# A two-block network in split precision: the first weight unit behind each norm of block 2 computed without the root

## The reference

```python
def modulate(x, g, shift, scale):
    return rmsnorm(x, g) * (1 + scale) + shift
for i in range(2):
    x   = x   + 0.5 * gt1 * swiglu(modulate(x, g1, sh1, sc1), ffn1_wi[i], ffn1_wo[i])
    ctx = ctx + 0.5 * cg1 * swiglu(modulate(ctx, g1, ch1, cs1), ffn1_wi[i], ffn1_wo[i])
    hx, hc = modulate(x, g2, sh2, sc2), modulate(ctx, g2, ch2, cs2)
    # i = 0: pointwise GLU, depthwise convolution of width 31, LayerNorm, swish, pointwise
    # i = 1: windowed attention of 16 query and 4 key heads with a sink; latent queries only
    x   = x + gt2 * y_lat            # (i = 0: ctx + cg2 * y_ctx too)
    x   = x + 0.5 * gt3 * swiglu(modulate(x, g3, sh3, sc3), ffn2_wi[i], ffn2_wo[i])
    # (i = 0: ctx too)
return rmsnorm(x, final_g)
```

## Time and profile before

| What | Value |
|---|---|
| Median of 3 runs | 3044.67 us (3044.47 to 3045.72) |
| Profiled execution | 3043.92 us |
| Its span, first to last instruction | 3042.1 us |
| PE busy | 2997.0 us, 99% |
| DVE busy | 2116.9 us, 70% |
| ACT busy | 1303.8 us, 43% |
| Mean granted TensorE clock | 0.998 |

### The profile page before, as it was taken

One profiled execution on the slowest core, in us unless ns is written; L12 is line 12 of the kernel. 1 busy time (PEld: TensorE's weight loads), 2 busy tenths in 40 slices (PEclk: granted clock), 3 DMA queues, 4 the chain that ended last, 5 costly groups with the idle time before them and its releaser, 6 DMA issues.

```text
span 3042.1 us, 48628 instructions
## 1 busy us (share of the span) xinstructions
PE 2997.0 (99%) x20580; PEld 2702.0 (89%) x20580; DVE 2116.9 (70%) x3302; ACT 1303.8 (43%) x1956; POOL 2.0 (0%) x5
## 2 busy tenths in 40 slices
PE   9999999999999999999999999999999999999999
PEld 9999999999999999998888865788888888886999
DVE  6668767767877766666678786666765677567655
ACT  5454555455455555454222332432224222246544
POOL 0000000000000000000000000000000000000000
PEclk9999999999999999999999999999999999999999
DMA  6554555645654555543444444234442344420453
GB/s 233 192 173 168 172 181 179 222 167 201 216 201 169 170 197 187 185 150 121 166 189 195 169 157 160 70 138 166 185 163 101 148 166 193 151 99 29 167 181 111
DMA packets 87784, 500.94 MB, mean 165 GB/s; under 512 B 15376, under 2 KB 20368, under 8 KB 33168
## 3 DMA queue, kind: packets, MB, share of 16 engines
q1 hardware_dynamic: 84880, 492.96, 44.9%
q10 hardware_dynamic: 2688, 4.88, 0.5%
HBM read 493.28 MB, written 3.36 MB: 163 GB/s over the span
## 4 chain that ended last, share of the span: by engine, by line
PE 89%; DVE 5%; ACT 2%; DVEq 1%; issue 1%; DMA 1%; ACTq 0%; SPq 0%
PE ps L709 28%; PE ps L711 28%; PE ps L710 27%; DVE wl L1845 1%; PE ps L1156 1%; ACT wh L1338 1%; DVE Hl L1837 1%; DVE XX L1837 1%; DVE Pp L1837 1%; PE ps L811 0%; PE ps L993 0%; ACT Hh L1445 0%; PE ps L864 0%; PE ps L700 0%; DVE ps L2612 0%
## 5 line engine op out<-in xcount | busy, mean ns | idle before, releaser
L1845 DVE TENSOR_TENSOR wl<-raw,wh 128x1024 fp32r<-128x1024 f32 (+2 forms) x779 | 919.5, 1184 | 622.6 <-ACT wh L1338 621.1
L1338 ACT ACTIVATE wh<-raw 128x1024 fp32r<-128x1024 f32 (+2 forms) x779 | 794.2, 1026 | 1295.4 <-PE ps L711 1261.9
L709 PE MATMUL ps<-Fh,wh 128*128 128x256 f32 (+1 forms) x3280 | 994.0, 303 | 7.5 <-DVE wl L1845 2.9
L710 PE MATMUL ps<-Fl,wh 128*128 128x256 f32 (+1 forms) x3280 | 989.0, 302 | 0.0
L711 PE MATMUL ps<-Fh,wl 128*128 128x256 f32 (+1 forms) x3280 | 989.0, 302 | 0.0
L709 PE MATMUL ps<-Hh,wh 128*128 128x256 f32 (+1 forms) x2576 | 866.9, 337 | 12.2 <-DVE Hl L1837 7.8
L711 PE MATMUL ps<-Hh,wl 128*128 128x256 f32 (+1 forms) x2576 | 856.2, 332 | 0.0
L710 PE MATMUL ps<-Hl,wh 128*128 128x256 f32 (+1 forms) x2576 | 856.2, 332 | 0.0
L709 PEld LDWEIGHTS ps<-Fh,wh 128*128 128x128 f32 x3280 | 626.7, 191 | 34.0 <-issue 5.7
L710 PEld LDWEIGHTS ps<-Fl,wh 128*128 128x128 f32 x3280 | 626.9, 191 | 22.4
L711 PEld LDWEIGHTS ps<-Fh,wl 128*128 128x128 f32 x3280 | 626.8, 191 | 22.4
(11 more groups left out here) (300 smaller groups left out, 1868.7 us busy)
## 6 DMA issues: line engine op xcount, KB each, us to landing
raw<-in_units SPq DMA_DIRECT2D x349, 1024.0 KB, 4.8
raw<-in_ada SPq DMA_DIRECT2D x72, 1024.0 KB, 6.8
raw<-in_units SPq DMA_DIRECT2D x32, 768.0 KB, 4.2
shifted<-u_rows SPq DMA_DIRECT2D x14, 284.5 KB, 4.8
shifted<-u_rows ACTq DMA_DIRECT2D x14, 284.5 KB, 5.5
QK<-in_conds SPq DMA_DIRECT2D x3, 1024.0 KB, 7.2
blocks<-in_taps SPq DMA_DIRECT2D x8, 384.0 KB, 8.1
raw<-in_units SPq DMA_DIRECT2D x10, 256.0 KB, 3.2
```

The costliest lines, as they stand in the source:

```text
L709: nc.tensor.matmul(o, wh[:, u.par, kc, w], xh(kc), start=(kc == 0), stop=False)
L710: nc.tensor.matmul(o, wh[:, u.par, kc, w], xl(kc), start=False, stop=False)
L1338: nc.scalar.activation(tile_of(wh[:, u.par], t, n), raw_tile(u, t), ACT.Copy) \
L1845: V.tensor_tensor(tile_of(wl[:, u.par], t, n), raw_tile(u, t), tile_of(wh[:, u.par], t, n).bitcast(F32), ALU.subtract).then_inc(lo_done, 1)
```

## The change

Hh and Hl get two more columns per chunk and stream, which hold the shift. The first unit behind a norm (`plain_unit`) runs on the high and low part of XX · S, without the root, and 258 columns wide, so that the last two columns give W · shift. One matmul holds 258 columns, so at n = 512 each of the 48 becomes two, one per stream, the context's in banks 5 and 6. The sums and the spreading of the root stand inside this unit, behind the first, second and third chunk's places; `norm_sums` and its fills are gone for norms 10 to 14. ACT then copies the root to SBUF (root_copy), and the normalised Hh and Hl are made as before, over the plain ones, and used from the second unit on; each high part waits until PE has read the plain chunk. At the eviction of unit 0 DVE multiplies each bank by the root (`times_root`) and the shift enters as a bias. The highs of XX · S are made on ACT behind the squares of each adding unit, the lows on DVE one adding unit later, ahead of the adds.

```diff
-Hh = sb("Hh", [P, 2, C, T], F32R)
+Hh_wide = sb("Hh_wide", [P, 2, C, T + 2], F32R)
...
+Hh, Hl = Hh_wide[:, :, :, 0:T], Hl_wide[:, :, :, 0:T]
...
+root_copy = Gb[:].rearrange("p c t -> p (c t)")[:, 1024:1536]
...
+    return 5 + t if s else 2 * u.par + t
...
+    def plain_unit(u, norm, n):
+        between = {(0, 0): lambda: sums(norm, False, n), (1, 0): lambda: sums(norm, True, n),
+                   (2, 1): lambda: spread_roots(4, number(norm), n)}
+        pe.wait_ge(lo_done, u.lo_done(1))
+        pe.wait_ge(banks_free[u.par], u.banks_free())
+        for kc in range(C):
+            for t in range(2):
+                if (kc, t) in between:
+                    between[kc, t]()
+                if t == 0:
+                    pe.wait_ge(plain_there, plain_chunk(norm, kc))
+                w = slice(P * t, P * t + P)
+                for s in range(n // T):
+                    o = ps[:, plain_bank(u, t, s), 0:T + 2]
+                    nc.tensor.matmul(o, wh[:, u.par, kc, w], Hh_wide[:, s, kc, :], start=(kc == 0), stop=False)
+                    nc.tensor.matmul(o, wh[:, u.par, kc, w], Hl_wide[:, s, kc, :], start=False, stop=False)
+                    mm = nc.tensor.matmul(o, wl[:, u.par, kc, w], Hh_wide[:, s, kc, :], start=False, stop=(kc == C - 1))
+                if kc == C - 1:
+                    mm.then_inc(mm_done, 1)
+            if kc < C - 1:
+                mm.then_inc(plain_read, 1)
...
-    def norm_sums(norm, n):
-        keep_busy(6, 4)
-        sums(norm, False, n)
-        keep_busy(6, 1)
-        sums(norm, True, n)
-        keep_busy(6, 5)
-        spread_roots(4, number(norm), n)
-        keep_busy(6, 6)
...
-                if kind == "G" and norm is None and g == 0 and i < 2:
+                if kind == "G" and fi > 4 and g == 0 and i == 0:
+                    plain_unit(u, norm_of(fi), n)
+                elif kind == "G" and fi > 4 and g == 0 and i == 1:
+                    linear(u, part(Hh, n), part(Hl, n), n, ready=h_ready(hn))
...
-        linear(Unit(K2_CONV + j), part(Hh, 512), part(Hl, 512), 512, ready=h_ready(3) if j == 0 else None)
+        if j == 0:
+            plain_unit(Unit(K2_CONV), 10, 512)
+        else:
+            linear(Unit(K2_CONV + j), part(Hh, 512), part(Hl, 512), 512, ready=h_ready(3) if j == 1 else None)
...
-    two_units(Unit(K2_KV), part(Hh, 512), part(Hl, 512), 512, h_ready(6), 2, second=value_products)
+    plain_unit(Unit(K2_KV), 13, 512)
+    u = Unit(K2_KV + 1)
+    pe.wait_ge(lo_done, u.lo_done(1))
+    pe.wait_ge(banks_free[u.par], u.banks_free())
+    for kc in range(C):
+        h_ready(6)(kc)
+        value_products(u, kc)
...
+        for kc in kcs:
+            for s in range(n // T):
+                ins = nc.scalar.activation(Hh[:, s, kc, :], (Xx, Xc)[s][:, kc, :], ACT.Copy, scale=scale_of(norm_i, kc, s))
+            ins.then_inc(plain_high, 1)
...
+            if norm_i < 15:
+                plain_highs(norm_i, n, (6 + t,))
...
+        if norm_i is not None:
+            act.wait_ge(rb_done, number(norm_i))
+            nc.scalar.activation(root_copy[:, 0:n], ps[:, 4, 0:n], ACT.Copy).then_inc(root_copied, 1)
         for kc in range(C):
+            if norm_i is not None and kc < C - 1:
+                act.wait_ge(plain_read, (norm_i - 10) * (C - 1) + kc + 1)
+            elif norm_i is not None:
+                act.wait_ge(mm_done, Unit(after).mm_done(1))
...
+                    act.wait_ge(rooted, fi - 3)
+                    for s in range(n // T):
+                        tok = slice(s * T, (s + 1) * T)
+                        ins = nc.scalar.activation(Tt[:, u.par, tok], Ss[:, tok], ACT.Silu, bias=shifted_by[:, s, 0:1])
...
+                        plain_highs(after, n, (2 * i, 2 * i + 1))
...
+            act.wait_ge(rooted, 1)
+            for s in range(2):
+                a, b = two(Ss[:])[:, s, :], two(Tt[:, u.par, :])[:, s, :]
+                nc.scalar.activation(a, a, ACT.Identity, scale=0.5, bias=shifted_by[:, s, 0:1])
+                ins = nc.scalar.activation(b, b, ACT.Tanh, scale=0.5, bias=shifted_by[:, s, 1:2])
+            ins.then_inc(turned, 1)
...
+    def plain_lows(norm_i, n, kcs):
+        for kc in kcs:
+            dve.wait_ge(plain_high, plain_chunk(norm_i, kc))
+            for s in range(n // T):
+                ins = stt(Hl[:, s, kc, :], (Xx, Xc)[s][:, kc, :], scale_of(norm_i, kc, s), Hh[:, s, kc, :].bitcast(F32),
+                          ALU.mult, ALU.subtract)
+            ins.then_inc(plain_there, 1)
...
+    def times_root(o, u, t, n):
+        for s in range(n // T):
+            tok = slice(s * T, (s + 1) * T)
+            ins = V.tensor_tensor(o[:, tok], ps[:, plain_bank(u, t, s), 0:T], root_copy[:, tok], ALU.mult)
...
+        dve.wait_ge(std_done, norm_i + 1)
+        V.reciprocal(Rr[:, 0:n // 4], Rr[:, 0:n // 4]).then_inc(rs_done, 1)
+        plain_lows(norm_i, n, (C - 1,))
+        lo(next_unit, 1)
+        dve.wait_ge(root_copied, norm_i - 9)
+        norm_parts(n, hn, gain, shift, root=root_copy)
...
+                    read_shifts(u, n)
+                    times_root(Ss, u, 0, n).then_inc(rooted, 1)
+                    times_root(Pp[:, u.par], u, 1, n)
+                    lo(u.later(2), 0)
+                    dve.drain()
+                    dve.wait_ge(tanh_done, done + 1)
+                    for s in range(n // T):
+                        p = Pp[:, u.par, s * T:(s + 1) * T]
+                        ins = stt(p, p, shifted_by[:, s, 1:2], Tt[:, u.par, s * T:(s + 1) * T], ALU.add, ALU.mult)
+                    ins.then_inc(banks_free[u.par], 1)
...
+                if last and i >= 1 and 10 <= after < 15:
+                    plain_pair(after, n, i - 1)
                 if last and i >= 2 and not summed_on_pe(after):
                     add_squares(after, i - 1, n)
...
+        if after < 15:
+            plain_pair(after, n, 2)
         dve.wait_ge(mm_done, u.mm_done(0))
         add_tile(u, 0, 6, n, gate).then_inc(half_added, 1)
         add_squares(after, 2, n)
...
+        if j == 0:
+            dve.wait_ge(mm_done, u.mm_done(1))
+            read_shifts(u, 512)
+            dve.drain()
+            for t in range(2):
+                stt(shifted_by[:, :, t], shifted_by[:, :, t], 0.5, tiny[:, 32 + C * t:33 + C * t].to_broadcast([P, 2]), ALU.mult, ALU.add)
+            times_root(Ss, u, 0, 512)
+            times_root(Tt[:, u.par], u, 1, 512).then_inc(banks_free[u.par], 1)
+            dve.drain().then_inc(rooted, 1)
         lo(u.later(2), 0)
-        dve.wait_ge(banks_free[u.par], u.read_out())
+        if j == 0:
+            dve.wait_ge(turned, 1)
...
-    V.tensor_copy(kraw, ps[:, 2 * u.par:2 * u.par + 2, :]).then_inc(banks_free[u.par], 1)
+    read_shifts(u, 512)
+    for t in range(2):
+        times_root(kraw[:, t], u, t, 512)
+    dve.drain()
+    for t in range(2):
+        for s in range(2):
+            k = kraw[:, t, s * T:(s + 1) * T]
+            ins = V.tensor_scalar(k, k, shifted_by[:, s, t:t + 1], None, ALU.add)
+    ins.then_inc(banks_free[u.par], 1)
...
```

89 lines of the change are left out of this document (71 added, 18 removed).

## The result

| | median | runs | profiled execution, span |
|---|---|---|---|
| before | 3044.57 us | 3041.49 to 3045.72 (4) | 3043.92, 3042.1 |
| changed | 3062.69 us | 3059.12 to 3067.89 (4) | 3067.89, 3066.1 |

The ratio is 1.0064, with a 95% interval of 1.0052 to 1.0076: the change costs 18 us by the medians, and 16 to 23 by the interval. The prediction said 3047.9 with a range to 3054.5. The direction of its sum was right, and the size was not. The profiled execution is the slowest of the four.

A forecast was written before the change was run, and what follows sets the result against it. PE, busy 99%, bounds the kernel; a norm's end depends on when its chunk chain starts. 6.2 - 1.6 - 1.7 - 0.5 + 0.7 = +3.1 on 3043.9 gives 3047.0, stated as 3047.9 for the median; range 3041.5 to 3054.5.

The forecast's parts named there:

- Something of the layout or the edit: Heading of Rival C: rows 258 elements apart slow matmuls on Hh or Hl, or the change does less; chance 0.10.
- the taps' 0.111 us: Time per convolution tap matmul on rows shifted by small offsets, taken as evidence against a layout cost.
- Rival C: Matmuls reading Hh or Hl 1 ns longer, 7.7 us, 3055.6; or plain unit kept waiting, 3055; chance 0.10.
- The adds' lateness: Ahead of norms 10 to 13: DVE's lows precede the adds, so tile 7's adds come 2.9 us late at norm 10.
- Norm 10: Norm before the convolution: first taps 4.7 us later, plus clock fall and matmul in flight; +6.2 us (+2 to +8).
- the clock's price: At norm 10's first taps: PE idles 10.9 us, the clock falls, and 48 tap matmuls cost 1.5 us more, plus 0.1.
- Norms 11 and 12: Norms before feed-forward units: the third unit starts earlier, giving -1.6 us and -1.7 us.
- Norms 13 and 14: Key rotation behind norm 13 starts earlier, -0.5 us; norm 14's third unit (n = 256) starts later, +0.7 us.
- rival B: PE's clock falls in the new short waits too, up to 1.6 us each at four more places; 3054.3 us, chance 0.18.
- the row of 2756 to 2758: Clock row of the kernel before: PE busy 0.14 us of 2, clock 1.00; held against rival B.
- The plain path as a whole: Sum of the terms of norms 10 to 14, nothing for the layout: +3.1 us.
- within 0.2%: Whole kernel: a change within 6.1 us, between 3038.6 and 3050.8, given a chance of 0.58.

The follow-up runs named there:

- e1: The kernel before with only the rows of Hh and Hl widened from 256 to 258 elements; 3060.67 us, ratio 1.0049.
- e4: The changed kernel with DVE's plain lows moved behind the adds, the last three chunks behind tile 7; 3058.63 us, ratio 1.0043.
- e13: The whole changed kernel on the layout of e12; 3073.55 us, ratio 1.0094.
- e12: The kernel before with rows of 258, each stream's piece of Hh and Hl beginning at a multiple of 8192 bytes; 3067.84 us, ratio 1.0077.
- e5: The changed kernel with rows of 256 and the shift in its own tile, 48 4-column matmuls at the plain unit's end; 3065.88 us.
- e15: e14 with old rows of 256, the shift in its own tile and 32 small matmuls spread over the plain unit; 3033.09 us, ratio 0.996.
- e17: The kernel before with only the convolution's unit 2 moved ahead of the taps of chunk 0; 3045.35 us, ratio 0.9995.
- e7: The kernel before with 256 bytes left free between Fl and the weight tiles; 3046.76 us (one run).
- e16: The kernel before with rows of 256, Hh and Hl interleaved by stream, streams 16384 bytes apart; 3047.17 us (one run).
- e18: The kernel before with Vb placed between Hh and Hl, so Hl lies 24576 bytes behind Hh; 3043.05 us (one run).
- e8: The kernel before with 128 bytes left free ahead of Hl and ahead of Fl; 3062.94 us, ratio 1.0055.
- e2: The kernel before with rows of 256 but the two streams 8256 bytes apart instead of 8192; 3067.91 us (one run).
- e10: e4 with fill matmuls in three PE waits: 88 ahead of the first taps, 22 each at norms 13 and 14; 3060.75 us.
- e11: e10 with the convolution's unit 2 ahead of the taps of chunk 0 in place of the 88 fills; 3043.90 us, ratio 1.000.
- e3: The kernel before with rows of Hh and Hl widened to 264 elements; 3057.61 us (one run).
- e9: The kernel before with rows of 258 elements and streams 8704 bytes apart; 3064.94 us (one run).
- e14: e11 on the layout of e12, with 10 fills instead of 22 in each wait of norms 13 and 14; 3049.34 us, ratio 1.0015.

## Why the prediction was wrong

- **The step that failed** is the sum's missing term for the rows of 258. The prediction counted nothing for the layout ("Something of the layout or the edit" had 0.10, at an assumed 1 ns for each matmul), and took the taps' 0.111 us as evidence against it. e1 measures 5.8 ns on every 512-column matmul that reads Hh or Hl, 15 us in all, against +3.1 for everything that the sum held; the taps are another form (32 outputs), read another tile and say nothing on it. Rival C named the cause, with half the cost (7.7 us, by 1 ns for each of 2576 x 3 matmuls where 1200 x 3 lose 5.8).
- **The adds' lateness**, 2.9 us by a round of 9.6 against 8.16 (its terms add up to 9.7): right in place, and 2.5 us in size; e4 shows that it's the order of the lows that makes it.
- **Norm 10**, +4.7 in the taps and a fall of the clock: the taps came 4.2 us later than before, and the idle time was right to 0.2 us; the clock's price was 1.6 and is 2.0 for the first taps (6.54 - 4.50). Against e1, same layout, norm 10 to norm 11 took 6.8 us more from t0 to t0 (212.1 against 205.3; 6.2 forecast, though 4.7 and 1.6 are 6.3). This stretch alone varies by up to 2.7 us between kernels with the order of before.
- **Norms 11 and 12**, -1.6 and -1.7: -2.4 and -2.3 against e1 (371.3 and 371.4 against 373.6), right in sign and more than forecast.
- **Norms 13 and 14**, -0.5 and +0.7: wrong, by a term put at nothing. From t0 to t0, and from norm 14's t0 to the end, they took 2.1 and 3.3 us more than in e1, and e13 took 0.6 and 2.4 more than e12. The starts were right (30.0 and 21.0), but rival B acts at both: 2.7 and 2.9 us without work put the clock to 0.50 for some 6 us. The prediction held the row of 2756 to 2758 against this, where the clock is still 1.00. It didn't look at the stretches behind it; four us later the same trace, of the kernel before, has:

```profile
2760.00:2762.00 2.00, 2.00 (x13) 1.67 (x13) 1.93 (x4) 0.71 (x4) 0.00 (x0) 0.50 0.00 0
```

So the wait that ends at 2757.86 (2.1 us) was followed by half the clock too: the fall can come while PE is already at work again. By the Trainium skill's page "TensorE: Matmul & The Clock Gate", section "HAM oscillation — how this bites in real kernels", a burst of matmuls starts cold behind a wait for DMA. The trace agrees at the taps, and behind the two waits for DVE, but not at norm 10's t0, where 1.6 us without work leave the clock at 1.00. The runs of one kernel differ in it: the two slower runs of the changed kernel (3067.89, 3065.01) have a mean clock of 0.994, the two faster (3059.12, 3060.36) of 0.996.
- **The plain path as a whole**, +3.1 in the sum (which makes 3047.8, not 3047.9, of 3044.67): 3.3 us by the changed kernel against e1 and 5.7 by e13 against e12, by medians, and from norm 10's t0 to the end 7.5 and 5.3 in the profiled executions. That 3.3 is near the forecast is luck, since norms 13 and 14 were off by 1 to 3 us each. Whether the forecast "within 0.2%" would have held without the layout isn't shown: the differences lie on both sides of 6.1 us, no run has the old rows and is otherwise the changed kernel, and e5 was spoiled.

## What to carry to other kernels

A buffer that many matmuls read shouldn't get a new row pitch for the sake of a few columns: try the layout alone first (one run here), and put the extra columns in a tile of their own, spread among wide matmuls. Work that is taken out of PE's way pays only where the freed time is given something to do: the plain path cost 6 us with PE idle ahead of the taps (e13 against e12). With the next unit moved into that gap, the lows behind the adds and 10 fills in two waits (e15) the kernel came out 12 us ahead, where the order of units alone gave nothing (e17). And inserted work belongs behind, not ahead of, what releases the next stage (e4). When a row with an idle engine is read for its clock, the rows behind it have to be read as well.

## What the hardware showed

- **Pitch and distance of moving operands.** Start to start of 512-column matmuls that read two runs of 256 columns, Hh and Hl:

| Kernel | row, bytes | streams apart | Hl behind Hh | spacing, us |
|---|---|---|---|---|
| before, e5 to e7, e15, e17 | 1024 | 8192 | 16384 | 0.2267 |
| e16 | 1024 | 16384 | 8192 | 0.2267 |
| e18 | 1024 | 8192 | 24576 | 0.2267 |
| e8 | 1024 | 8192 | 16512 | 0.2333 |
| e2 | 1024 | 8256 | 16512 | 0.2355 |
| changed, e1, e4, e10, e11 | 1032 | 8256 | 16512 | 0.2325 |
| e3 | 1056 | 8448 | 16896 | 0.2325 |
| e9 | 1032 | 8704 | 17408 | 0.2342 |
| e12 to e14 | 1032 | 16384 | 32768 | 0.2342 |

The cheap ones are those in which all rows lie at multiples of 1024 bytes from one another. Their own place doesn't decide: in e1 and e2 Fh and Fl start 256 bytes further than before, with their rows unchanged to one another, and stay at 0.2267. 256-column matmuls are a little shorter in the slow layouts, 0.118 to 0.119 against 0.120 behind norm 14. What in the memory does it stays open. In e12 chunk 0 lies at a multiple of 8192 bytes from Hh's start in all four pieces and is as slow as the mean (0.235), chunks 1 and 5 are the slowest (0.237) and chunks 3 and 7 the least slow (0.230); in e8 the same distances cost less on Fh and Fl (0.2289). Whether rows of 258 at any placing could be cheap wasn't tried beyond e12.
- **The clock falls under a busy PE too.** In e5 PE was busy without a gap, but mostly with 4-column matmuls from 1972.04 on, and the granted clock went from 1.00 to 0.50, the level of 1.2 GHz. The same kind of matmul, one or two at a time between wide ones, left it at 1.00 (e15).
- **The fall can come behind the wait.** In the kernel before it came between 2759 and 2760, 1 to 2 us after a wait of 2.1 us had ended (another 0.5 us without work lies between); in e4 between 2732 and 2733, about 1 us after the rotation had started behind 2.7 us without work. With 10 fills of 0.225 us in the waits of norms 13 and 14 the clock stayed at 1.00 (e14).
